# One ordinary chunk instead of two ahead of the seven-product chunks, and a constants load moved to chunk 4

## The reference

```python
def swiglu(x, w_gate, w_up, w_down):
    return (jax.nn.silu(x @ w_gate) * (x @ w_up)) @ w_down

f = swiglu(rms_norm(h, ffn1_norm_pre[l]), ffn1_w_gate[l], ffn1_w_up[l], ffn1_w_down[l])
h = h + 0.5 * rms_norm(f, ffn1_norm_post[l])
```

## Time and profile before

| | us |
|---|---|
| median of three runs | 2223.87 |
| the three runs | 2218.61, 2223.87, 2225.46 |
| the profiled execution, its own time | 2224.23 |
| its span | 2222.3 |

### The profile page before, as it was taken

The page is one execution under the profiler, slowest core; times in us unless marked ns, Lnnn a source line. Parts: engine busy times, 40 slices in busy tenths (PEclk is TensorE's granted clock), DMA queues, the critical chain, the costliest instruction groups (busy, mean ns, idle before and its releaser), DMA issues.

```text
span 2222.3 us, 33977 instructions
## 1 busy us (share of the span) xinstructions
PE 2149.3 (97%) x14857; PEld 1319.8 (59%) x14858; DVE 852.8 (38%) x1404; ACT 375.5 (17%) x812; POOL 93.1 (4%) x106
## 2 busy tenths in 40 slices
PE   8999999999999999999988999999999999999997
PEld 7677786888677765677877533444444444344432
DVE  3666692531344444367777521111211121111113
ACT  1000201140111122344333110001110010000000
POOL 1000000000000011122111000000000000000000
PEclk9999999999999999999999899999999999999998
DMA  9597774244435460000022689999999999999996
GB/s 350 191 309 254 264 259 158 88 148 164 171 114 170 144 227 19 3 3 3 22 51 98 265 362 426 423 427 425 425 425 427 425 425 425 419 423 426 426 426 261
DMA packets 153877, 581.63 MB, mean 262 GB/s; under 512 B 9556, under 2 KB 108700, under 8 KB 120704
## 3 DMA queue, kind: packets, MB, share of 16 engines
q1 hardware_dynamic: 149744, 564.70, 64.7%
q0 software_dynamic: 3568, 12.72, 1.7%
q10 hardware_dynamic: 416, 2.01, 0.2%
HBM read 578.32 MB, written 3.43 MB: 262 GB/s over the span
## 4 chain that ended last, share of the span: by engine, by line
PE 88%; DVE 5%; DMA 3%; issue 1%; SPq 1%; ACT 1%; POOL 0%; DVEq 0%; POOLq 0%
PE ps L2786 22%; PE ps L2794 11%; PE ps L689 10%; PE ps L855 8%; PE ps L741 6%; PE ps L1546 4%; PE ps L2765 3%; PE ps L2827 3%; PE ps L991 2%; PE ps L963 2%; PE ps L1875 2%; PE ps L1895 1%; PE ps L1977 1%; PE ps L1165 1%; DMA arena<-in_w 1%
## 5 line engine op out<-in xcount | busy, mean ns | idle before, releaser
L2786 PE MATMUL ps<-ring,const 128*64 128x512 f32 (+1 forms) x1536 | 473.1, 594 | 0.1
L2786 PEld LDWEIGHTS ps<-ring,const 128*64 128x64 f32 (+1 forms) x1536 | 160.4, 144 | 305.1 <-issue 304.9
L2786 PE MATMUL ps<-arena,const 128*64 128x512 f32 (+1 forms) x512 | 225.7, 593 | 0.0
L3025 DVE TENSOR_SCALAR arena<-ps 128x1024 f32<-128x1024 f32 x18 | 22.0, 1225 | 469.5 <-PE ps L2786 469.5
L2794 PE MATMUL ps<-ring,const 128*64 128x512 f32 (+1 forms) x768 | 190.4, 594 | 0.9 <-DMA ring<-in_w 0.9
L689 PE MATMUL ps<-ring,arena 128*128 128x256 f32 x800 | 183.4, 380 | 1.2 <-DVE arena L813 1.2
L855 PE MATMUL ps<-arena,ring 128*128 128x256 f32 x800 | 173.1, 379 | 0.0
L855 PEld LDWEIGHTS ps<-arena,ring 128*128 128x128 f32 x800 | 151.9, 190 | 20.7
L689 PEld LDWEIGHTS ps<-ring,arena 128*128 128x128 f32 x800 | 150.0, 190 | 21.9 <-DVE arena L813 2.4
L741 PE MATMUL ps<-ring,arena 128*128 128x512 f32 x352 | 154.7, 592 | 0.0
L2794 PEld LDWEIGHTS ps<-ring,const 128*64 128x64 f32 (+1 forms) x768 | 65.6, 143 | 112.4 <-issue 110.9
(11 more groups left out here) (515 smaller groups left out, 2612.9 us busy)
## 6 DMA issues: line engine op xcount, KB each, us to landing
ring<-in_w SPq DMA_DIRECT2D x96, 2048.0 KB, 19.7
ring<-in_w SPq DMA_DIRECT2D x96, 1024.0 KB, 17.5
arena<-in_w SPq DMA_DIRECT2D x32, 2048.0 KB, 20.3
ring<-in_w_in SPq DMA_DIRECT2D x26, 1536.0 KB, 7.1
arena<-in_w SPq DMA_DIRECT2D x32, 1024.0 KB, 19.8
ring<-in_w_ada SPq DMA_DIRECT2D x16, 1536.0 KB, 8.9
ring<-in_ffn_w_gate SPq DMA_DIRECT2D x44, 512.0 KB, 5.0
ring<-in_ffn_w_up SPq DMA_DIRECT2D x44, 512.0 KB, 6.1
```

Of the source, the lines that this page charges most:

```text
L2786: ins = pe.matmul(ps[a * n:(a + 1) * n, q, :], xsT[:, k, a * n:(a + 1) * n], chunk(chunks[a])[:, q * 512:(q + 1) * 512], start=False, stop ...
```

## The change

Two edits. The number of ordinary chunks of f1 goes from 2 to 1, and ACT issues the constants load after the second silu of chunk 4 instead of chunk 0.

```diff
-PLAIN = {"f1": 2, "f2": 1}
+PLAIN = {"f1": 1, "f2": 1}
...
         def beside_first_act(a):
             def at_step(c):
-                if c == 0:
-                    const_rest_act(a)
                 if c == 1:
                     in2_act(a)
+                if c == 4:
+                    const_rest_act(a)
             return at_step
```

## The result

| | us |
|---|---|
| before, median of ten runs | 2222.16 |
| changed, median of ten runs | 2227.38 (2223.86 to 2230.97) |
| ratio changed to before | 1.0022, 95% interval 1.0013 to 1.0030 |
| changed, the profiled execution: time and span | 2229.84, 2228.0 |

The change costs 0.22%, 4.9 us with an interval of 2.9 to 6.7 (the two medians are 5.2 apart). A loss of over 0.3%, to which the prediction gave 0.52, was not measured.

The account below looks back on a forecast made before the run. PE, busy for 97% of the span, was taken to bound the kernel. Terms 5.4 - 1.8 + 1.7 - 0.2 + 2.0 = +7.1 us put the profiled execution at 2231.3 and the median at 2231.0, range 2226.5 to 2235.

Parts of the forecast that it names:

- A loss of over 0.3%: Whole kernel: the changed kernel measurably slower, by more than 0.3% (6.7 us); chance 0.52.
- The wait for the mix, +5.4: Chunk 0 of f1: PE's transposes wait for L828 behind chunk 1's mix, starting at 33.13 instead of 27.73; +5.4 us.
- One product fewer, -1.8: Chunk 1 of f1: seven products instead of eight, 12.53 us instead of 14.32; -1.8 us.
- The clock, +1.7: After PE's 6.3 us gap at chunk 0: clock at its lower level for 3.4 us, PE doing half its work; +1.7 us.
- The 0.18 us at chunk 2, -0.2: Chunk 2 of f1: PE's 0.18 us wait goes away, as DVE is then ahead of PE; -0.2 us.
- The constants in the first 45 us, 0: Start of f1: slots 5 to 7 land up to 5 us earlier without the constants, but nobody waits for them; 0.
- The constants at chunk 4, +2.0: Chunk 4 of f1: moved load leaves some 2.0 us of DMA backlog reaching chunk 7's loads; +2.0 us, bounds 0 and 4.9.
- The shift reaches the end in full: Behind f1: weight loads are gated by PE, which carries the shift, so all +7.1 us reach the end time.
- a part of the shift being given back: Rival, behind f1: where something other than PE's progress sets a start, leaving +1 to +4 us, 2225 to 2228; chance 0.08.
- The signs that the prediction named for being right: Trace of f1: L800 near 27.3, L732 near 33.1, low clock, down product near 47.5, constants near 109, chunk 6 or 7 wait.

Follow-up runs that it names:

- products alone: The kernel before with only the first edit: one ordinary chunk in f1, constants left at chunk 0; ratio 1.0011 to before.
- mix behind: The changed kernel with the mix of chunk 1 behind chunk 0's two multiplications on DVE instead of ahead of them; ratio 1.0010 to the kernel before.
- gap filled: The changed kernel with 24 unused identity matmuls between chunk 0's products and its transposes, where PE waits; ratio 1.0015 to the kernel before.
- constants alone: The kernel before with only the second edit: constants load at chunk 4, two ordinary chunks; ratio 1.0009 to before.
- second traces: Single repeated executions of the changed kernel and of the kernel before, nothing altered; 2228.53 and 2220.66 us.
- Changed, bias later: The changed kernel with POOL's two large attention bias transfers held back until the second silu of chunk 9; ratio 0.9999 to the kernel before.
- pure delay: The kernel before with 72 unused identity matmuls between chunk 0's products and its transposes, as a known delay of PE; ratio 1.0070 to before.

## Why the prediction was right, and where it was not

**The wait for the mix, +5.4.** Right in mechanism, shown by "products alone" and "mix behind". Measured +4.84 in the first pair of traces: the slot landed at 26.87 instead of 27.24, and the two L828 took 0.75 together instead of 0.88. Against the eight traces in which chunk 0 is as before (27.18 to 28.50) the five with the gap (32.14 to 32.98) lie 4.6 later on average.

**One product fewer, -1.8.** Right: 1.7 with the gap filled.

**The clock, +1.7.** Right in size: 1.9, by filling the gap (14.46 to 12.59). The step was not as told. The prediction took one low stretch of 3.4 us, all of it on a busy PE; in the traces it is 6.8 us long and the first half falls into the gap, where it costs nothing, so that the size agrees by luck. The four traces with the open gap bear this out: the low stretch begins at 29.6 to 30.2 and lasts 6.8 us in each, what is left of it when PE starts again is 3.5 to 4.8 us, and chunk 1 loses half of that, 1.7 to 2.3 us (14.30 to 14.93 against 12.59).

**The 0.18 us at chunk 2, -0.2.** Wrong. The wait is there again at 61.77. DVE's mix ended at 53.5, but the copies of L922 wait for PE (0.71 us, for L902, behind the down product), `ada_dve` starts behind them and behind a result of ACT (0.47 us), and so `base` comes as late as PE does. Some 0.3 us came back in chunk 3 instead.

**The constants in the first 45 us, 0.** Right: the mix of chunk 2 started 1.7 us earlier in "constants alone", and chunk 1 and 2 took as long as before.

**The constants at chunk 4, +2.0.** The size was near (2.3 to 3.6 in the traces), the step was not, so that its nearness is luck. The text put the cost at chunk 7, with the backlog reaching its loads, and said of chunk 6 that what is lost there "is not added". In the trace the last load of chunk 7 lands at 153.62, 5.0 us later than before, while PE is by then 11.0 us later (4.66 + 6.34); the mix of chunk 7 starts at 155.28 right behind L828, without a wait. Chunk 6 pays it all: 6.34 us, less the 3.36 that chunk 7 no longer waits, +3.0; +2.5 between the second traces of both kernels, +3.6 in "constants alone", and +2.3 between "products alone" and the changed kernel over both traces. What I missed is that the bias chain starts while the backlog is there. With some 3 us of backlog by the prediction's sum the last load of chunk 6 came 6.0 us later (136.4, against 125.8 plus the shift of 4.66): from 121.90 on the weights share the DMA with POOL's 2304 KB, which is the likely reason that it is more than the backlog. "Changed, bias later" and "products alone" show that it takes both: without the chain, or without the constants, chunk 6 waits for nothing and its last load takes 10.4 or 10.8 us instead of 17.4. And the waiting (1.24 and 2.92 us) brought the clock down, another 1.7 us of the 6.34. The size belongs to this one alignment: without the constants in the way the same load took 13.2 us in the first trace of before, 14.3 in the second and 15.1 with the pure delay.

The Trainium skill, page "DMA: Bandwidth & Descriptors", section "Queues, rings and completion order", says that each DMA engine takes turns between the queues that have work. By that rule a queue that is late when another one starts is slowed again for as long as both have work; the trace agrees (17.4 us to landing against 13.2 before, and 10.4 with the chain held back).

**The shift reaches the end in full.** Not borne out for this change. At the end of f1 the sum should have been +7.1 and was +7.64, and +7.6 between the means of two traces each. Yet the time rose by 4.9 (2.9 to 6.7): of what PE had lost at the end of f1, 0.9 to 4.7 us did not arrive. This step, and not the sum of the terms, is why the end time lies 2.2 us under the forecast; the prediction had given 0.08 to a part of the shift being given back. For all six kernels with one ordinary chunk the ratio gives 1.2 to 3.9 us less than the mark at the end of f1; for the five others it gives from 1.6 us less to 0.4 more, and the pure delay of 16.05 us came out as 15.6. So it is not a rule that delays are given back, and chance alone is a poor reason. Where it happens these runs don't settle: the part behind is 1991.9 us on average in the seven traces with one ordinary chunk and 1992.9 in the seven with two, with a spread of 1989.4 to 1997.6 for one and the same code.

Some of that spread can be read off. Two long stretches are alike in all fourteen traces whatever came before them: the first to the last L828 of the second feed-forward part takes 194.34 or 194.35 us, and from there to the first L2210 it is 138.4. What differs is 146.2 to 149.8 us from the last record of f1 to the attention (first L1073), 227.9 to 229.6 from there to that feed-forward part, 325.6 to 332.1 in the recurrence of the second block (first L2210 to first L2650), and 944.2 to 946.6 behind it. The first of these goes with the clock behind the 2.7 us wait of the earlier trace rows: 146.2 us in the four traces in which it stayed at 1.00, 147.3 to 147.6 in the eight with 3.4 us at the lower level, 148.5 in the one with 6.8, 149.8 in the one with 10.2. The recurrence does not follow it: with the clock low in the same places it took 328.9 us in the first trace of before and 325.6 in "mix behind". One trace per kernel is a sample of all this. So the terms can be read from marks in f1 to about half a microsecond, the end to 3 only.

The signs that the prediction named for being right are in the trace: L800 at 26.97 released by a DMA, the down product at 47.03, the constants' issue at 108.27, a wait in chunk 6 that was not there before, and f1's end 7.64 us later. Of the five terms two are right in step and size (the wait for the mix, the saved product), two agree in size by luck (the clock, the constants), and the small one at chunk 2 is wrong; why not all of their sum reached the end stays open.

## What to carry to other kernels

An early start of work pays nothing if it stands, on an engine that runs in order, ahead of something that another engine waits for and has to wait itself for a transfer: read off when its data land and what is queued behind it, before counting the work that it saves. A load that is moved into idle DMA time must leave no backlog when the next burst of another queue begins, and not only fit in on average. And where the end scatters by more than the effect, compare marks at the end of the stage that was touched: repeated traces agreed there within 0.3 us, while the intervals of the ratios, with ten runs or so, are 0.1% to either side. Such a mark is not the end time, though: here about a third of the shift at the mark was missing in it.

## What the runs showed of the hardware

The clock fell behind much shorter waits than the 6 us gap. In "mix behind" waits of 0.93 and 2.40 us were followed by 0.50 for 3.4 us; in "products alone" a single one of 1.96 was, while the wait of 1.84 of before was not. The same wait of 2.7 us behind f1, in all fourteen traces, with a second one of 1.2 to 1.4 us 2 to 4 us behind it, was followed by a low stretch of 0, 3.4, 6.8 or 10.2 us. A low stretch on a busy PE costs half its length (1.7 to 2.3 us in chunk 1, for 3.5 to 4.8 us at the lower level), so a wait of 2 us can cost nearly 4: chunk 7 of "products alone" took 16.43 us instead of 12.53.
